# Last feed-forward stage: three plain panels ahead of the seven-product ones, other banks for two small products, splits ahead of sums

## The reference, cut to what matters

```
h = h + 0.5 * g3 * swiglu(modulate(h, norm_ffn2, sh3, sc3), w_ffn2_in, w_ffn2_out)
return rmsnorm(h, final_norm)
# swiglu: a, b = split(x @ w_in); (silu(a) * b) @ w_out        x 512 x 1024, w_in 1024 x 5632, w_out 2816 x 1024
# modulate: rmsnorm(x, w) * (1 + scale) + shift                scale, shift, g3: products of silu(c) with w_mod
```

## Time and profile before

| | before |
|---|---|
| median of 3 runs | 3058.93 us |
| the profiled execution | 3061.42 us, span 3059.3 us |
| TensorE busy | 3009.3 us (98% of the span) |
| VectorE, ScalarE, GpSimd busy | 1610.3, 1097.9, 287.2 us |
| mean granted TensorE clock | 0.995 |
| f3, first matmul to last | 2687.2 to 3047.2 us of the span |

### The profile page before, as it was taken

How to read it: one execution, slowest core, us unless ns; L and a number is a source line. 1 busy time by engine, 2 the same in 40 slices (tenths; PEclk the granted TensorE clock), 3 DMA queues, 4 the chain that set the end, 5 groups by cost and what they waited for, 6 DMA issues and landing times.

```text
span 3059.3 us, 36737 instructions
## 1 busy us (share of the span) xinstructions
PE 3009.3 (98%) x15582; PEld 2466.6 (81%) x15582; DVE 1610.3 (53%) x2393; ACT 1097.9 (36%) x1639; POOL 287.2 (9%) x223
## 2 busy tenths in 40 slices
PE   8999999999999999999999999999999999989998
PEld 6767888877667888878888888888888888779997
DVE  4565333354654334363223325677777784476666
ACT  4553222234533232242212124343333425354444
POOL 0233000020332000010000001010101021000000
PEclk9999999999999999999999999999999999989999
DMA  5113442222125322211111213121212133312222
GB/s 185 44 56 152 179 154 94 99 95 76 42 98 200 131 98 90 102 69 56 69 60 62 79 40 112 42 100 47 98 55 92 57 117 111 124 63 104 98 102 76
DMA packets 45059, 285.20 MB, mean 93 GB/s; under 512 B 5135, under 2 KB 5663, under 8 KB 19424
## 3 DMA queue, kind: packets, MB, share of 16 engines
q1 hardware_dynamic: 42480, 269.77, 24.7%
q0 software_dynamic: 2416, 13.09, 1.2%
HBM read 277.04 MB, written 5.79 MB: 92 GB/s over the span
## 4 chain that ended last, share of the span: by engine, by line
PE 93%; DVE 4%; ACT 2%; POOL 1%; issue 1%; DMA 0%; DVEq 0%; SPq 0%; POOLq 0%; ACTq 0%
PE ps L814 26%; PE ps L815 25%; PE ps L816 25%; PE ps L1066 2%; PE ps L1068 2%; PE ps L1067 2%; PE ps L905 2%; PE ps L984 2%; PE ps L997 1%; PE ps L1011 1%; PE ps L890 1%; DVE CA L2286 1%; DVE wlo L1836 1%; PE ps L836 1%; PE ps L837 0%
## 5 line engine op out<-in xcount | busy, mean ns | idle before, releaser
L814 PE MATMUL ps<-A1h,whi 128*128 128x512 f32 x1920 | 761.7, 397 | 8.4 <-DVE A1l L1855 7.3
L815 PE MATMUL ps<-A1l,whi 128*128 128x512 f32 x1920 | 748.6, 390 | 0.0
L816 PE MATMUL ps<-A1h,wlo 128*128 128x512 f32 x1920 | 748.6, 390 | 0.0
L1836 DVE TENSOR_TENSOR wlo<-wraw,whi 128x2048 fp32r<-128x2048 f32 (+2 forms) x221 | 464.9, 2103 | 248.6 <-ACT whi L1290 248.6
L1290 ACT ACTIVATE whi<-wraw 128x2048 fp32r<-128x2048 f32 (+2 forms) x221 | 385.3, 1744 | 484.9 <-PE ps L816 452.0
L814 PEld LDWEIGHTS ps<-A1h,whi 128*128 128x128 f32 x1920 | 361.7, 188 | 90.2 <-issue 14.2
L816 PEld LDWEIGHTS ps<-A1h,wlo 128*128 128x128 f32 x1920 | 360.8, 188 | 76.4
L815 PEld LDWEIGHTS ps<-A1l,whi 128*128 128x128 f32 x1920 | 361.4, 188 | 72.9 <-issue 2.2
L2012 DVE TENSOR_TENSOR SIL<-SIL,ps 128x512 f32<-128x512 f32 (+1 forms) x88 | 54.7, 621 | 452.9 <-PE ps L816 369.9
L1549 ACT ACTIVATE SIL<-ps 128x512 f32<-128x512 f32 (+1 forms) x88 | 47.9, 544 | 547.5 <-PE ps L816 545.6
L2286 DVE SCALAR_TENSOR_TENSOR CA<-YIN,vec,CA 128x512 f32<-128x512 f32 x238 | 192.0, 807 | 6.9
(11 more groups left out here) (435 smaller groups left out, 5454.1 us busy)
## 6 DMA issues: line engine op xcount, KB each, us to landing
wraw<-wstream SPq DMA_DIRECT2D x159, 1024.0 KB, 4.8
MW<-wstream SPq DMA_DIRECT2D x34, 1024.0 KB, 6.4
wraw<-wstream SPq DMA_DIRECT2D x42, 768.0 KB, 4.2
wraw<-wstream SPq DMA_DIRECT2D x34, 640.0 KB, 3.9
wraw<-wstream SPq DMA_DIRECT2D x4, 960.0 KB, 4.7
hk<-gd POOLq DMA_DIRECT2D x1, 2560.0 KB, 15.8
X<-xT SPq DMA_DIRECT2D x4, 512.0 KB, 7.0
sx<-X POOLq DMA_DIRECT2D x1, 2048.0 KB, 7.7
```

The lines of the kernel that those rows point to most:

```text
L814: mm(o, l[0], r[0], start=start, stop=False)
L815: mm(o, l[0], r[1], start=False, stop=False)
L816: return mm(o, l[1], r[0], start=False, stop=stop)
L1836: tt(wlo[i_ % 2][:, 0:n], wraw[i_ % 2][:, 0:n], raw(whi[i_ % 2][:, 0:n]), SUB).then_inc(ev("lo", i_).by(dve_wlo), 1)
```

## The change

It does six things. (1) Three tiles of f3 are plain instead of two. (2) `mods("ffn2")` takes its banks from `OB`. (3) The split of the token sums (`T3h`, `T3l`) moves from ahead of the loop over tiles into it: on ScalarE behind the silu of tile 0, on VectorE behind the `wlo` split that stands at j == 1. (4) Of a seven-product panel only 1536 of 2048 columns are split. (5) At f == 6 VectorE does the `wlo` split of the next group's first panel before its quarter sums. (6) The load that overwrites a seven-product panel also waits for that panel's last quarter sum.

```diff
-SEVEN = {"f3": 2}
+SEVEN = {"f3": 3}
...
+        def split_width(i):
+            return 1536 if stream[i]["quarters"] else width(i)
...
             def mods(*point):
-                ring = OB if point[0] in ("f0", "f1", "f3") else AB
+                ring = OB if point[0] in ("f0", "f1", "ffn2", "f3") else AB
...
             def prep(i):            # on ScalarE and on VectorE
-                    i_, n = todo[0], width(todo[0])
+                    i_, n = todo[0], split_width(todo[0])
...
-                for k in range(0, 8, 4):        # ScalarE, ahead of the loop
-                    e.wait_ge(ev("tokens", name, 3 if k else 1), PB.of("modp", 35).full)
-                    act(T3[0][:, k:k + 4, :], B3[:, k:k + 4, :], ACT.Copy, ...)
...
                         if j < SEVEN[name]:
                             silu(j)
+                            for k in range(0, 8 if j == 0 else 0, 4):
+                                e.wait_ge(ev("tokens", name, 3 if k else 1), PB.of("modp", 35).full)
+                                act(T3[0][:, k:k + 4, :], B3[:, k:k + 4, :], ACT.Copy, ...)
...
-                for k in range(0, 8, 4):        # VectorE, ahead of the loop
-                    e.wait_ge(ev("tokens hi", name, k // 4))
-                    tt(T3[1][:, k:k + 4, :], B3[:, k:k + 4, :], raw(T3[0][:, k:k + 4, :]), SUB)...
...
                         at("gu", name, j)
+                        if j == 1:
+                            for k in range(0, 8, 4):
+                                e.wait_ge(ev("tokens hi", name, k // 4))
+                                tt(T3[1][:, k:k + 4, :], B3[:, k:k + 4, :], raw(T3[0][:, k:k + 4, :]), SUB)...
...
                     for f in range(0, 8, 2):
+                        at("down", name, g, f)
                         if f == 6 and g < 3:
                             mix(leader[name, g + 1])
-                        at("down", name, g, f)
-                        if f == 6 and g < 3:
                             mixed_low(leader[name, g + 1])
...
             def load(i):
-                    e.wait_ge(ev("lo", i - 2))
+                    e.wait_ge(ev("lo", i - 2), ev("mixed", *stream[i - 2]["key"][1:], 3) if stream[i - 2]["quarters"] else None)
```

More of the change, by code:

```diff
@@ L1495, in seed_up @@
                     act(u.ap[:, 0:256], u.ap[:, 256:512], ACT.Copy, bias=0.0, scale=1.0).then_inc(ev("up seeded", name, j).by(act_out), 1)
-                for k in range(0, 8, 4):
-                    e.wait_ge(ev("tokens", name, 3 if k else 1), PB.of("modp", 35).full)
-                    act(T3[0][:, k:k + 4, :], B3[:, k:k + 4, :], ACT.Copy, bias=0.0, scale=1.0).then_inc(ev("tokens hi", name, k // 4).by(act_out), 1)
                 for g, js in enumerate(HIDDEN):
@@ L1505, in seven @@
                             silu(j)
+                            for k in range(0, 8 if j == 0 else 0, 4):
+                                e.wait_ge(ev("tokens", name, 3 if k else 1), PB.of("modp", 35).full)
+                                act(T3[0][:, k:k + 4, :], B3[:, k:k + 4, :], ACT.Copy, bias=0.0, scale=1.0).then_inc(
+                                    ev("tokens hi", name, k // 4).by(act_out), 1)
                             if after:
@@ L2069, in seven @@
                 stt(out=b21, in0=b22, scalar=-1.0, in1=b21, op0=MUL, op1=SUB).then_inc(ev("tokens", name, 3).by(dve_out), 1)
-                for k in range(0, 8, 4):
-                    e.wait_ge(ev("tokens hi", name, k // 4))
-                    tt(T3[1][:, k:k + 4, :], B3[:, k:k + 4, :], raw(T3[0][:, k:k + 4, :]), SUB).then_inc(ev("tokens lo", name, k // 4).by(dve_out), 1)
                 for g, js in enumerate(HIDDEN):
@@ L2082, in seven @@
                         at("gu", name, j)
+                        if j == 1:
+                            for k in range(0, 8, 4):
+                                e.wait_ge(ev("tokens hi", name, k // 4))
+                                tt(T3[1][:, k:k + 4, :], B3[:, k:k + 4, :], raw(T3[0][:, k:k + 4, :]), SUB).then_inc(
+                                    ev("tokens lo", name, k // 4).by(dve_out), 1)
                         if j < SEVEN[name]:
```

## The result

Four runs of the changed kernel took 3039.05, 3039.74, 3041.04 and 3041.08 us, median 3040.39 us, against 3058.88 us (four runs, 3058.57 to 3059.39): ratio 0.9939, 95% interval 0.9922 to 0.9956, 18.5 us less. The forecast was 3040.5 us. The profiled execution is one of the four, 3039.74 us, span 3037.6 us.

The account below looks back on a forecast made before the run. TensorE, busy 98% of the span, was taken as the bound; gains only from its waits, clock or matmul count. Terms -13.45 + 0.55 + 0.8 + 0 - 6.35 = -18.45 us, from 3058.93 to 3040.5 us; range 3036.5 to 3046.5.

Parts of the forecast that it names:

- The bank: Start of tile 0: freeing bank 0 from the turned row lets TensorE begin early, so tile 1 starts 13.45 us earlier.
- Rival B: Tile 0: the bank is not what holds it, or something else does until VectorE is through; 3053.4 us, chance 0.03.
- Tile 2's wait: Ahead of tile 2: moved token splits share the queues, so TensorE waits for panel 2's wlo, +0.55 us.
- The exchange of a panel: Third plain tile: one panel runs in plain form instead of as seven products, +0.8 us.
- The opening: Start of the seven products: the loss around the E3l wait moves from tile 2 to tile 3 and stays, 0 us.
- rival D: Start of the seven products: the clock does not fall there; 3037.7 us, chance 0.12.
- The group heads: First panel of later groups: wlo ahead of the quarter sums removes TensorE's waits, gaining 6.35 us.
- Rival A: Tile 0: the clock falls because TensorE starves between input chunks; 3048.4 us, chance 0.07.
- Rival C: Ahead of tile 1 or tile 2: one more fall of the clock behind a wait; 3043.3 us, chance 0.14.
- Rival E: Inside the groups: VectorE falls behind and each seven-product panel waits for the E3 split; 3065.2 us, chance 0.03.
- The narrower split: Seven-product panels: ScalarE and VectorE save 0.4 and 0.5 us per panel, which TensorE does not see.
- SyncE's added wait: A group's first panel: the load comes 0.4 us later, covered by about 9 us, so it costs nothing.

Follow-up runs that it names:

- experiment 3: Kernel before with only the group-head edits: wlo split ahead of the quarter sums, 1536 columns split, the load's added wait; 3053.89 us.
- experiment 2: Changed kernel with the old banks for the two modulation products and the turned row; 3054.63 us.
- experiment 1: Kernel before with one edit, the two modulation products and the turned row in banks 4 to 7; 3049.06 us.
- experiment 6: Changed kernel with the two modulation products back in the old ring and only the turned row moved, from bank 0 to bank 2; 3041.37 us.
- experiment 4: Changed kernel with all 2048 columns split instead of 1536; 3042.62 us.
- experiment 7: Changed kernel with two plain tiles instead of three and the token split on VectorE at j == 0; 3041.84 us.
- experiment 5: Changed kernel with the E3 split ahead of silu (ScalarE) and the gate product (VectorE) on the last plain tile; 3037.32 us.

## Why the prediction was right

The mechanism and the sum held. Profile against profile the move is 3061.42 - 3039.74 = 21.7 us, more than the 18.45 forecast; the difference has one main source, the opening.

- **The bank.** Forecast 13.45 us between the two starts of tile 1. Measured 2700.35 - 2686.59 = 13.76 us, of which 0.29 us is that the whole stage begins earlier in this execution (2672.17 against 2672.46 for the first chunk): 13.47 us. The prediction took the old start of tile 1 from the trace, and with it a cost that it did not name: the lower clock behind the 14.6 us of idle, 13.14 us for a tile that needs 10.9. It is part of what the bank cost, and it varies: 13.4 us in the profile of experiment 3, 14.0 in that of experiment 2. That it is the bank, and of the three products the turned row alone, is shown by experiments 1, 2 and 6. Rival B falls with them.
- **Tile 2's wait.** 0.55 us forecast, 0.5 us measured (2698.11, against tile 1's last matmul at 2697.38 + 0.23).
- **The exchange of a panel.** The 11.01 us of tile 2 stand against 10.08 us for a seven-product panel; with the 0.1 us pause at a panel's first matmul taken off, 0.8 us, as forecast.
- **The opening.** The idle time is as forecast (2.8 us; 2.7 before). The term was put at 0, and between these two executions it was -2.6 us, for the clock: 0.71 in the earlier trace rows, 1.00 after. That is rival D, in this one execution. In the profiles of experiments 2, 3, 4 and 6, with a wait of 2.5 to 2.7 us in the same place, the same 48 matmuls took 10.6 to 10.8 us at a mean clock of 0.84: between the two. The term of 0 leaned on one profile of the kernel before, which had the lowest clock of the six.
- **The group heads.** 6.35 us forecast. Counted by distances between starts, 1.75 + 1.76 + 3.96 = 7.5 us were lost before and 0.8 us after (0.3 for the `wlo`, 0.1 for the seed, 0.4 for `E3l`; forecast 0.2, 0.3, 0.3, and 0.1 for the next panel, which did not come). Experiment 3 gives 5.35 us in the timed runs, near the 4.8 us that were expected there if the clock mostly holds at the fourth head. So in the medians this term is about a microsecond smaller than was forecast from the profile, and something makes up for it: the clock at the opening and the clock in tile 0 before are the candidates that the profiles show, and no run separates them. That the medians agree to 0.1 us is partly luck. The lower bound of this term was also worked out wrongly: 6.35 - 4.8 is a gain of 1.55 us, not nothing.
- **Rival A** did not come: with 11.33 busy of 12.37 us during tile 0 the clock stayed at 1.00, as in the earlier trace rows for the earlier emission, and it did so in the six other profiles in which tile 0 starts early. The Trainium skill's rule on short idle times between groups ("TensorE: Matmul & The Clock Gate", "A second HAM failure mode: psum-queue depth-cycling") finds no case here. **Rival C** did not come in this profile, with 1.00 over tiles 1 and 2. **Rival E** did not come either: VectorE takes the later E3 split without a wait in the second and third group.

The parts do not add up one by one: the banks alone give 10.2 us, all but the banks 4.6 us (3059.24 - 3054.63), together 14.8 of 18.5 us. The rest belongs to both: starting tile 0 early is worth 3.7 us more when the token splits and the third plain tile keep VectorE's work from being due at tile 2. The profile of experiment 1 shows where: the wait of 5.4 us there and a mean clock of 0.67 over the 9.3 us behind it. The narrower split, which I costed at nothing in the steady panels and used only in the heads' sum, is worth 2.2 us in experiment 4: its profile shows 2.1 us at the heads (0.6, 0.6 and 1.25, less the 0.3 that was left) and 0.5 us in small pauses at the panels behind them. SyncE's added wait was taken back by no experiment of its own; in the profile after, no wait of TensorE inside the groups exceeds 0.4 us.

## What to carry to other kernels

A long wait whose named releaser is a tiny operation is worth following to the bank or buffer: the waiting instruction needed nothing of that operation but the room it read from, and a ring that takes the oldest place can put a side product just where the next large one is pinned. When such a wait goes, count at once which queue is late next; here what stood ahead of tile 2 held back 3.7 of 14 us. And where an engine ends up behind a sum, put the part that its first instruction needs ahead of the sums, and look on both queues for an order that is only written so: two moved calls gave 3.1 us, and two more 1.8 us.

## What the runs showed of the hardware

The fall of the clock behind a wait of TensorE is not the same from run to run. What the ten profiles show:

- behind 14.6 us ahead of tile 0 it fell in all three (tile 0 at a mean of 0.86, 0.79 and 0.84);
- behind 4.9 and 5.4 us ahead of tile 2 it fell in both (0.50 over `first` in experiment 7, 0.52 over the 6.4 us behind the wait in experiment 1);
- behind 2.5 to 2.8 us at the opening it fell in five of six: 0.71 in the kernel before, 0.84 in experiments 2, 3, 4 and 6, and 1.00 in the changed kernel. In experiments 4 and 6 the matmuls right behind the wait still ran at full pitch, and the slow ones began 1.1 and 1.5 us after it;
- behind 2.2 us at the fourth head it fell to 0.54 in the kernel before and stayed at 1.00 in experiment 1;
- behind 1.5 us (1.65 us lost) at the other two heads, four times in these two profiles, it did not fall.

Where the clock falls, the price varies too. The kernel of experiment 2, which starts tile 0 after 14.6 us of idle and keeps the opening, spread from 3052.06 to 3056.25 us in 11 runs, that of experiment 5, without either, from 3036.46 to 3037.63 us in 5. That the clock makes this spread is a likely reading, not a shown one.
